# A streaming encoder step on one core: the last mixer's small fills, the rounding of a weight tile and the start of the output projection are placed later

## What is computed

```python
h = jnp.einsum('btd,de->bte', rms_norm(x, g_attn), w_in)     # q, k, v of mixers A, B, C, D
oa = stick_breaking(qa, ka_all, va_all)       # 4 heads, all the past
ob = window_sink(qb, kb, vb)                  # 4 q heads, 2 kv heads, own chunk + 2 before
oc = differential(qc, kc_all, vc_all)         # 4 heads, two halves each, all the past
od = chunk_band(qd, kd, vd)                   # 4 heads, own chunk + 8 before
x = x + concat(oa, ob, oc, od) @ w_out
xn = rms_norm(x, g_ffn)
x = x + (silu(xn @ w_gate) * (xn @ w_up)) @ w_down
y = rms_norm(x, g_final)                      # and the new key and value rows are stored
```

## Time and profile before

| | |
|---|---|
| runs | 1499.99, 1503.12, 1498.17 us; median 1499.99 |
| profiled execution | 1497.65 us, its span 1495.9 us |
| TensorE | 1448.4 us busy, 97% of the span |
| VectorE, ScalarE, GpSimd | 690.1 (46%), 417.5 (28%), 272.6 us (18%) |
| DMA | 75.91 MB, mean 51 GB/s |
| chain that ended last | TensorE 91%, VectorE 3%, ScalarE 2% |

### The profile page before, as it was taken

How to read it: one execution, slowest core, us unless ns; L and a number is a source line. 1 busy time by engine, 2 the same in 40 slices (tenths; PEclk the granted TensorE clock), 3 DMA queues, 4 the chain that set the end, 5 groups by cost and what they waited for, 6 DMA issues and landing times.

```text
span 1495.9 us, 23065 instructions
## 1 busy us (share of the span) xinstructions
PE 1448.4 (97%) x8862; PEld 1281.2 (86%) x8862; DVE 690.1 (46%) x1267; ACT 417.5 (28%) x1036; POOL 272.6 (18%) x428
## 2 busy tenths in 40 slices
PE   5999999999999989999999999999999999999997
PEld 4988887777878867778989899999999998989895
DVE  6335754666625345445452525344444434352516
ACT  4223445554546666533101010101000000101013
POOL 6224654433422112225000000000000000000002
PEclk9999999999999999999999999999999999999998
DMA  5321102100021123010411101011111111100003
GB/s 177 112 71 47 29 16 75 42 17 15 15 75 33 35 70 123 19 54 6 136 57 29 56 28 56 28 56 42 42 46 40 55 55 29 56 28 28 0 0 134
DMA packets 90481, 75.91 MB, mean 51 GB/s; under 512 B 5672, under 2 KB 83017, under 8 KB 90397
## 3 DMA queue, kind: packets, MB, share of 16 engines
q1 hardware_dynamic: 90412, 75.00, 16.4%
HBM read 64.06 MB, written 10.77 MB: 50 GB/s over the span
## 4 chain that ended last, share of the span: by engine, by line
PE 91%; DVE 3%; ACT 2%; POOL 1%; issue 1%; DMA 1%; SPq 0%; DVEq 0%; POOLq 0%; ACTq 0%
PE acc L794 25%; PE acc L796 24%; PE acc L795 24%; PE acc L941 5%; PE acc L965 3%; PE acc L1003 3%; PE acc L987 2%; PE acc L809 1%; PE acc L1111 1%; DVE low_z L1433 1%; DMA x_in<-in_x_prompt_dram 1%; DVE acc L1436 1%; PE acc L860 0%; PE acc L879 0%; DVE prob_slot L1457 0%
## 5 line engine op out<-in xcount | busy, mean ns | idle before, releaser
L794 PE MATMUL acc<-ohi,gu_hi 128*128 128x384 f32 (+1 forms) x1056 | 345.0, 327 | 1.8 <-issue 1.8
L796 PE MATMUL acc<-ohi,gu_lo 128*128 128x384 f32 (+1 forms) x1056 | 344.9, 327 | 0.0
L795 PE MATMUL acc<-olo,gu_hi 128*128 128x384 f32 (+1 forms) x1056 | 344.6, 326 | 0.0
L1313 ACT ACTIVATE silu<-acc 128x384 f32<-128x384 f32 (+1 forms) x66 | 31.2, 473 | 640.1 <-PE acc L796 640.1
L794 PEld LDWEIGHTS acc<-ohi,gu_hi 128*128 128x128 f32 x1056 | 198.8, 188 | 2.7 <-issue 2.2
L795 PEld LDWEIGHTS acc<-olo,gu_hi 128*128 128x128 f32 x1056 | 198.9, 188 | 0.4
L796 PEld LDWEIGHTS acc<-ohi,gu_lo 128*128 128x128 f32 x1056 | 198.8, 188 | 0.0
L1570 DVE TENSOR_TENSOR prod<-acc,silu 128x384 f32<-128x384 f32 (+1 forms) x66 | 35.4, 536 | 338.2 <-ACT silu L1313 338.2
L1590 DVE TENSOR_TENSOR x<-acc,x 128x512 f32<-128x512 f32 x198 | 134.5, 689 | 69.1 <-PE acc L796 64.4
L1640 POOL TENSOR_SCALAR meansq<-sumsq 128x1 f32<-128x1 f32 (+1 forms) x27 | 9.5, 352 | 802.8 <-ACT sq_junk L1139 770.6
L794 PE MATMUL acc<-xhi,win_hi 128*128 128x384 f32 (+1 forms) x384 | 132.1, 344 | 6.7 <-POOL xlo L1649 3.6
(11 more groups left out here) (206 smaller groups left out, 2436.9 us busy)
## 6 DMA issues: line engine op xcount, KB each, us to landing
win_raw<-in_w_in_dram SPq DMA_DIRECT2D x22, 512.0 KB, 3.9
gu_raw<-in_w_gate_dram SPq DMA_DIRECT2D x22, 512.0 KB, 3.9
gu_raw<-in_w_up_dram SPq DMA_DIRECT2D x22, 512.0 KB, 4.7
down_raw<-in_w_down_dram SPq DMA_DIRECT2D x22, 512.0 KB, 3.9
x_in<-in_x_prompt_dram SPq DMA_DIRECT2D x8, 512.0 KB, 6.9
wo_raw<-in_w_out_dram SPq DMA_DIRECT2D x8, 512.0 KB, 4.4
x<-in_x_prompt_dram SPq DMA_DIRECT2D x8, 512.0 KB, 4.7
out_dram<-y_out SPq DMA_DIRECT2D x8, 512.0 KB, 2.6
```

The source lines that it names most:

```text
L794: pe.matmul(out, a_hi, b_hi, start=first, stop=False)
L795: pe.matmul(out, a_hi, b_lo, start=False, stop=False)
L796: return pe.matmul(out, a_lo, b_hi, start=False, stop=last)
L1313: act.activation(silu[:, q % 2, 0:n], bank(2 * (q % 2), n), ACT.Silu).then_inc(silu_done, 1)
```

## The change

The small fills `rows` (tiles 7, 8) and `vr` (three) of mixer B leave the list of mixer D. What is left of that list is spread over mixer D's first 17 pairs (54 to 70). The five are spread as a list of their own, the `vr` first, over the 18th pair of mixer D and the first two of mixer B (71 to 73). Weight tile 4 is rounded two rounds after the last fill of its slab and no longer one. The output projection's first product is in round B0 + 2 = 74, and a memset on VectorE that stood ahead of it moves along. SP's wait for outputs 12 to 14 and its last two loads of x move to round B0 + 6.

```diff
--- before.py
+++ after.py
@@ -172,14 +172,14 @@
                 done += 1
         yield from small[done:]
 
-    def stand(new, mixer):
+    def stand(new, mixer, among=slice(None)):
 
 
         new = list(new)
         if mixer is None:
             where = [[] for _ in new]
         else:
-            own = [r for r in range(len(pairs)) if pairs[r][0].mixer == mixer]
+            own = [r for r in range(len(pairs)) if pairs[r][0].mixer in mixer][among]
             free = [room(pairs[r][0]) for r in own]
             rest = (sum(f.cost for f in new) - sum(free)) / len(own)
             until, total = [], 0.0
@@ -214,8 +214,8 @@
            *mixed(project("D"), [*rows("C", (8,)), *cached("C"), *biases("D")]), *values("D", [0])], "C")
     stand([*mixed(values("D", range(1, NT)), rows("D", *pairs_of_tiles[2:4])),
            *mixed(project("B"), [*rows("D", (8,)), *cached("D"), *biases("B")]),
-           *cached("B"), *mixed(values_by_columns("B"), [*rows("B", (7,), (8,)), *values_turned("B", (0, 1, 2))]),
-           *values_turned("B", (3, 4, 5), (6, 7, 8))], "D")
+           *cached("B"), *values_by_columns("B")], "D", slice(17))
+    stand([*values_turned("B", (0, 1, 2), (3, 4, 5), (6, 7, 8)), *rows("B", (7,), (8,))], "DB", slice(17, 20))
     return fills, slabs, place
 
 
@@ -596,9 +596,9 @@
         O_SPLITS += [(B0 + 10, 2, 0), (B0 + 10, 3, 0), (B0 + 16, 2, 1), (B0 + 16, 3, 1), (NR + 4, 2, 2), (NR + 4, 3, 2)]
 
         OUT = [(j, half) for j in (5, 2, 3, 4, 6, 7, 8, 0, 1) for half in range(2)]
-        OUT_SPOT = [(B0 + 1 + k, 1) for k in range(18)]
+        OUT_SPOT = [(B0 + 2 + k, 1) for k in range(18)]
         wo_round = [spot[slab_last[s]][-1][0] for s in (19, 20, 21)]
-        WO_SPLITS = [(first_pair["D"] + 6, 5), (wo_round[0] + 2, 0), (wo_round[1] + 2, 1), (wo_round[2] + 1, 4),
+        WO_SPLITS = [(first_pair["D"] + 6, 5), (wo_round[0] + 2, 0), (wo_round[1] + 2, 1), (wo_round[2] + 2, 4),
                      (B0 + 5, 6), (B0 + 6, 7), (B0 + 7, 2), (OUT_SPOT[-1][0] + 1, 3)]
 
         def low_round(at):
@@ -739,6 +739,8 @@
                     load_wo(6)
 
                     load_x1(range(6, NT))
+                if r == B0 + 6:
+
                     sp.wait_ge(o_split, 14)
                     load_x1(range(2))
 
@@ -1501,7 +1503,7 @@
                 for s in range(NSLAB):
                     if split_round[s] == r:
                         split_win(s)
-                if r == B0 + 1:
+                if r == B0 + 2:
                     dve.wait_ge(o_split, 12)
                     dve.memset(x1[DEC:P, NT - 1], 0.0)
                 for k in out_at(r):
```

## The result

The changed kernel takes 1514.72 us (median of 4 runs, 1512.88 to 1516.26), against 1499.87 of the kernel before in the same runs: ratio 1.0096, 95% interval 1.0075 to 1.0117, 1.0% slower. The forecast was 1518.4, slower; its range holds the time, and the size is 3.7 us too large.

A forecast was written before the change was run, and what follows sets the result against it. TensorE was taken as the bound nearly everywhere, ScalarE holding it at the hand-over. First output product 19.3 us late (2.6 of it from Parts 1 to 3), -1.4 and +0.5 from Part 5: +18.4, 1518.4 us; range 1508 to 1522.

The forecast's parts named there:

- Part 4: Pair 73: ScalarE's second k_rows copy waits for a store queued behind nine loads; first output product at 576.0, 19.3 us late.
- only issued behind it: Rival: the k_rows store is issued after the burst but not held by it, landing in 1.6 us: +9.7, 1509.7; chance 0.17.
- Part 1: Pairs 65, 67, 68, 69: late turns without a half fill as cover cost 1.2 us each, less a 0.4 wait: +4.4.
- Part 2: Pair 70: its small fill and the 2.7 us k_rows wait go, an uncovered late turn costs 1.2: -1.5 us.
- Part 3: Pairs 71 to 73, to mixer D's last values: weight tile 4's rounding leaves, v_B waits grow by 0.8: -0.3 us.
- Part 5: Output products: first as slow as before (0), work between first and second now ahead (-1.4), weight tile 3 wait (+0.5).
- the clock stays low longer: Rival: after the stall the second output product runs slow too, 2.5 us more: 1520.9; chance 0.12.
- Faster: Rival: ScalarE no longer holds TensorE in the hand-over from mixer D to B, 7.6 us of waits go: 1492.4; chance 0.04.

The follow-up runs named there:

- e1: Changed kernel with the rows of mixer B's last tile copied to a second area of k_rows, without waiting for the store before: 1499.49 us, ratio 1.0003.
- e2: Changed kernel with the two late rows fills ahead of the three vr fills, still one k_rows area: 1499.87 us, ratio 1.0009.
- e6: Changed kernel with all nine loads of the burst issued one round later, behind the stores of k_rows: 1500.31 us, ratio 1.0010.
- e10: Changed kernel with the store of tile 7's rows issued from ScalarE's own DMA queue, not SP's: 1504.07 us, ratio 1.0049.
- e5: Changed kernel with three of the burst's nine loads issued one round later, behind the store of k_rows: 1511.03 us, ratio 1.0075.
- e8: e7 with one half fill of pair 65 also put behind the late turn: 1494.16 us, ratio 0.9976.
- e9: Kernel before the change, with the second k_rows area for mixer B's last tile as its one edit: 1499.81 us, ratio 1.0002.
- e4: Kernel before the change, with the output products and the memset of x1 starting in pair 74, not 73: 1500.14 us, ratio 1.0010.
- e11: Changed kernel with weight tile 4 rounded in the round where the kernel before has it: 1513.35 us, ratio 1.0103.
- e3: Kernel before the change, with the second half fills of pairs 67 to 70 ahead of the late turn: 1500.58 us, ratio 1.0013.
- e7: e1 with the second half fills of pairs 67 to 70 put back behind the late turn: 1496.73 us, ratio 0.9982.

## Why the prediction was right or wrong, point by point

- **Part 4, the store behind the burst: right**, and the term that decides: +16.8 measured, +16.7 forecast. From the burst's first issue to the store's landing 15.2 us, where 15.5 was taken from the earlier trace rows. That it fits to 0.1 us is luck: with the same nine loads ahead it was 13.8 to 16.4 us in five executions, and 0.3 less here is made up by 0.3 more for what follows the landing (1.4 and not 1.1). e1 shows that the net loss is this wait, e2 and e6 that it is the order, and e10, with SP's own store behind the burst and ScalarE's past it, that it is the queue. e5 agrees with a price by the bytes, but is too small a step to show it alone. The rival "only issued behind it" (1509.7) is out: it had the store take 1.6 us from issue, and it took 9.8. The Trainium skill's price of one DMA ("DMA: Bandwidth & Descriptors", "Anatomy of one DMA"), an estimated 2.2 us here, is near the mark only with nothing of the burst ahead (1.6 in e6), and the forecast was right not to sum by it. That descriptors are consumed in ring order on each DMA engine, from the same page's "Queues, rings and completion order", agrees with e5 and e6.
- **Part 1, the uncovered late turns: right in kind, mis-sized.** "Without cover a pair pays 2.28 - 1.10 = 1.2 us" took its 2.28 from pair 63, where four short transposes stand in the place; they were left in the price of the wait. In the changed kernel a pair with nothing there takes 2.08 (518.34 to 520.42, with the two gaps shown below), so the price is 0.98, and by the table of e8 it is 0.86 to 0.91 in the four pairs, 3.55 in all and not 4.8. That is 1.25 of the 1.7 us by which +4.4 missed +2.7. Most of the rest is in pair 69, which is 0.28 shorter in e8 than before: its small fill (rows of tile 7) is gone, one of the transposes "left out" in the forecast.

```profile
518.34 1.03 PE L967 MATMUL acc<-ident,prob_slot_D 128*128 128x128 f32 x8
519.70 0.30 PE L967 MATMUL acc<-ident,prob_slot_D 128*128 128x128 f32 x1 [0.33 <-ACT probs_t_D L1257]
520.19 0.30 PE L967 MATMUL acc<-ident,prob_slot_D 128*128 128x128 f32 x1 [0.19 <-ACT probs_t_D L1257]
520.42 1.35 PE L943 MATMUL acc<-kT_D,qT_D 64*128 64x512 f32 x8
```

The forecast also said that the new waits would show as "about a microsecond" each. They don't: TensorE's label is on 0.33 + 0.19 us of it, and the remainder is the copies' and turns' own alternation. A reader who looks at the list of waits alone finds 2.8 us in eleven pieces and misses half of the price.
- **Part 2, pair 70: right**, -2.1 against -1.5; the late turn that took over cost 0.6 and not 1.2, as the table of e8 shows. e9 confirms that the wait that went was ScalarE's queue.
- **Part 3: right in size** (+0.1, forecast -0.3, bounds -1.1 to +1.0), by pieces that cancel. The waits fell further than forecast: 1.8 us for v_B where 1.5 + 0.8 was taken, and where the last values waited 3.0 they wait for nothing now, while pair 70's values wait 1.4. In all 3.1 us in place of 4.5. The clock took it back, in part at least: it was at the lower level (0.50) from 551 us on, in the kernel before only from 555. e10, the same work up to there, had it fall only at 554, and from scores 71 to values 71 it took 10.33 us in place of 10.87. The forecast had no term for that.
- **Part 5: one piece wrong.** The first output product was to "run as slowly as before: 0". It took 4.55 us (574.74 to 579.29), not 5.28: its first products ran at the lower of the two levels (granted clock 0.50 until 578), and the clock was back before its last three. The rival "the clock stays low longer" (1520.9) did not happen: the second product, from 580.60, ran at full clock. The clock was already low before the stall (0.56 in the 10 us ahead, against 0.77), so the stall had little to take away. What the Trainium skill has in "TensorE: Matmul & The Clock Gate", "Loop structure matters more than you think", matmuls cold behind a wait and warm when they follow each other, agrees with this trace (0.50 behind the stall, full clock before the first product's end); the slow second product was the rival's own step. The wait for the low half of weight tile 3 was 0.6 against 0.5 in this execution, 0.5 in e6, 0.2 in e4 and e11; the timing can't tell it from nothing. TensorE's row for it:

```profile
664.64 0.50 PE L796 MATMUL acc<-wo_hi,ohi 128*128 128x512 f32 x1 [0.55 <-DVE wo_lo L1526]
```

- **The sum.** Against +18.4 stand +15.9 behind pair 64 in the profiled execution and +14.85 of the medians. 1.7 of the difference is part 1, 0.6 part 2, 0.7 the first product, less 0.4 of part 3. The last 1.0 lies between one execution and the median; the section below shows what such an execution gains or loses outside the change.
- **"Faster" at 0.04**: the change alone couldn't be faster, but its idea could. e8 shows that the mechanism named there (ScalarE no longer holding TensorE in pair 70) is worth something once the store isn't in the way and the copies have cover, the two conditions that the rival named.

## What to carry to other kernels

A buffer that is written again only after its store has landed is safe just as long as the store is issued ahead of the big loads of its queue: before moving work past a burst of loads, look at what each queue has ahead of the stores that somebody waits for, and count the megabytes ahead at the full queue's rate as a first estimate, not one transfer's latency. A second area, the store ahead of the burst, or the burst behind the store each take it away; another queue only in part. And when a planner is called on a shorter list, look at where it now puts all the other items: here that cost 2.7 us, and five halves put back gave 4.1. And when two single profiles are compared, compare the granted clock of the stretch first: in e3 it was a third of the difference.

## What was not expected of the hardware

**The same instructions at the same place run at either level of the clock, from one execution to the next.** e6 and the changed kernel have the same order of work up to pair 73. Stretch 410 to 420 us, pairs 54 and 55, e6 first, the changed kernel second:

```profile
410.00:420.00 10.00, 8.32 (x73) 7.33 (x70) 5.24 (x17) 4.55 (x20) 5.06 (x11) 1.00 0.18 53
```
```profile
410.00:420.00 10.00, 8.32 (x58) 7.53 (x57) 3.84 (x15) 4.16 (x18) 4.27 (x10) 0.83 0.18 53
```

TensorE is as busy in both, but the granted clock is 1.00 in one and 0.83 in the other; between 414 and 418 us it was at the lower level (0.50) in part. Of the 13 profiled executions of this study six show it (e1, e2, e7, e9, e10 and the changed kernel). It costs 1.5 us there: from the scores of pair 54 to those of pair 55 it took 6.63 us in e6 (413.89 to 420.52) and 8.14 in the changed kernel (412.46 to 420.60), and none of it was made up by pair 64 (481.59 and 481.65). The stretches 10 to 40, 700 to 740 and 1480 to 1490 us do the same in some executions. The kernel before has 1.00 there, e9, which is the kernel before up to pair 70, has 0.83. A single profile can therefore be some us off in places that a change doesn't touch; I took differences only from pair 64 on, so that this fall is not in them; the one from 540 to 546 us, in e3 and e9 alone, is in e3's.

**A store from a second queue went past most of a full queue, but took 6.1 us for 64 KB,** against 9.8 in the same queue and 1.6 on its own (e10).
